# Two-block transformer step on one core: second output projection rescheduled, first gate/up pair by plain products

## The reference

```python
mixed = jnp.concatenate([rms_norm_2(attn, attn_out_norm[l]),
                         rms_norm_2(sgu, sgu_out_norm[l])], axis=-1)
y = mixed @ w_out[l]                       # 1024 x 1024 by 1024 x 1024
x = x + rms_norm_2(y, post_mix_norm[l])
h = rms_norm_2(x, pre_ffn_norm[l])
f = (jax.nn.silu(h @ w_gate[l]) * (h @ w_up[l])) @ w_down[l]   # D_FF = 2816
x = x + rms_norm_2(f, post_ffn_norm[l])
```

## Time and profile before

| | us |
|---|---|
| median of 3 runs (lowest to highest) | 2106.87 (2106.09 to 2108.21) |
| the profiled execution's own time | 2106.91 |
| its span, first to last instruction | 2105.1 |
| PE busy | 2011.8 (96% of the span) |
| DVE, POOL, ACT busy | 1333.3, 955.3, 844.4 |
| mean granted TensorE clock | 0.978 of full |

### The profile page before, as it was taken

How to read it: one execution, slowest core, us unless ns; L and a number is a source line. 1 busy time by engine, 2 the same in 40 slices (tenths; PEclk the granted TensorE clock), 3 DMA queues, 4 the chain that set the end, 5 groups by cost and what they waited for, 6 DMA issues and landing times.

```text
span 2105.1 us, 27422 instructions
## 1 busy us (share of the span) xinstructions
PE 2011.8 (96%) x10009; PEld 1667.0 (79%) x10009; DVE 1333.3 (63%) x1759; ACT 844.4 (40%) x1349; POOL 955.3 (45%) x566
## 2 busy tenths in 40 slices
PE   7999999999999999999998998876999999999997
PEld 6888888888887778888887798755888888878885
DVE  7887777665547554973512544797656565656977
ACT  5444444434420044650203765456333323324443
POOL 1344555323334397733541101776555555535552
PEclk8999999999999999999999999987999999999998
DMA  9223322111112152341112001022333233347344
GB/s 285 63 79 111 111 74 94 52 38 30 50 52 80 41 190 91 120 142 59 41 30 80 1 1 51 21 100 70 105 120 102 79 118 105 100 168 242 100 137 153
DMA packets 178924, 193.96 MB, mean 92 GB/s; under 512 B 9799, under 2 KB 122904, under 8 KB 178842
## 3 DMA queue, kind: packets, MB, share of 16 engines
q1 hardware_dynamic: 172420, 178.53, 26.8%
q10 hardware_dynamic: 6422, 14.37, 1.9%
HBM read 151.71 MB, written 41.16 MB: 92 GB/s over the span
## 4 chain that ended last, share of the span: by engine, by line
PE 78%; DVE 10%; ACT 5%; issue 4%; POOL 2%; DMA 1%; SPq 0%; DVEq 0%; ACTq 0%; POOLq 0%
PE psum L1491 7%; PE psum L1493 6%; PE psum L1492 6%; PE psum L960 6%; PE psum L962 6%; PE psum L961 6%; PE psum L1121 3%; PE psum L1402 3%; PE psum L1559 3%; PE psum L1561 3%; PE psum L1560 3%; PE psum L980 3%; PE psum L981 3%; PE psum L982 3%; PE psum L1391 2%
## 5 line engine op out<-in xcount | busy, mean ns | idle before, releaser
L756 POOL TENSOR_TENSOR w_hi<-w_raw,ones 128x1024 fp32r<-128x1024 f32 x60 | 149.2, 2487 | 481.5 <-PE psum L962 357.2
L960 PE MATMUL psum<-h_hi,w_hi 128*128 128x512 f32 x704 | 284.1, 404 | 0.0
L962 PE MATMUL psum<-h_hi,w_lo 128*128 128x512 f32 x704 | 274.8, 390 | 0.0
L961 PE MATMUL psum<-h_lo,w_hi 128*128 128x512 f32 x704 | 274.3, 390 | 0.0
L1591 ACT ACTIVATE arena<-psum 128x1024 f32<-128x1024 f32 (+7 forms) x135 | 100.8, 750 | 220.5 <-PE psum L962 135.3
L759 POOL TENSOR_TENSOR w_lo<-w_raw,w_hi 128x1024 fp32r<-128x1024 f32 x60 | 163.9, 2732 | 4.7
L961 PEld LDWEIGHTS psum<-h_lo,w_hi 128*128 128x128 f32 x704 | 132.4, 188 | 28.4 <-issue 2.6
L960 PEld LDWEIGHTS psum<-h_hi,w_hi 128*128 128x128 f32 x704 | 132.4, 188 | 28.4 <-issue 2.6
L962 PEld LDWEIGHTS psum<-h_hi,w_lo 128*128 128x128 f32 x704 | 132.1, 188 | 28.5
L1559 PE MATMUL psum<-w_hi,h_hi 128*128 128x512 f32 x308 | 121.5, 394 | 7.8 <-DVE h_lo L3032 5.1
L1560 PE MATMUL psum<-w_lo,h_hi 128*128 128x512 f32 x308 | 121.1, 393 | 0.0
(11 more groups left out here) (414 smaller groups left out, 5298.0 us busy)
## 6 DMA issues: line engine op xcount, KB each, us to landing
w_raw<-w_in SPq DMA_DIRECT2D x64, 512.0 KB, 3.9
act_op<-arena SPq DMA_DIRECT2D x77, 256.0 KB, 2.1
arena<-act_op SPq DMA_DIRECT2D x77, 256.0 KB, 2.7
w_raw<-w_gate SPq DMA_DIRECT2D x22, 512.0 KB, 4.0
w_raw<-w_up SPq DMA_DIRECT2D x22, 512.0 KB, 5.2
arena<-ada_w SPq DMA_DIRECT2D x16, 512.0 KB, 7.2
arena<-w_out SPq DMA_DIRECT2D x16, 512.0 KB, 5.6
out_T<-arena SPq DMA_DIRECT2D x16, 512.0 KB, 5.9
```

What stands on the lines that cost most here:

```text
L960: pe.matmul(o, wh, xh, start=(k == 0), stop=False)
L961: pe.matmul(o, wh, xl, start=False, stop=False)
L962: return pe.matmul(o, wl, xh, start=False, stop=(k == KT - 1))
```

## The change

It edits one stretch of the kernel, in six places.

1. **Attention scale.** The eight tiles are shared: DVE takes the even ones, ACT the odd ones. The root's table is loaded by ACT beforehand, and the first four B high parts go ahead of the wait for the attention output.
2. **B side eight places ahead.** `q_b2` has eight slots, ACT makes the B high part of step n+4 when it makes the A high part of step n. POOL's queue changes: T4 (four) and then S1 (four) both follow the low part of step 7, where S1 had been spread over steps 4 to 7 and T4 over 8 to 11; S4 moves from steps 18 to 21 to steps 22 to 25.
3. **A side order.** `Q_ORDER_A` makes the A parts of steps 26, 24, 27, 25 (operand A12, known early) between those of 16 and 20.
4. **Last two products tile by tile.** Steps 20 to 27 (P3 and P2) run per token tile: 12 matmuls of P3, then 12 of P2. Tile t then has C12 and C11 after 24 (t+1) matmuls.
5. **Norm of tokens.** New queues for ACT and DVE (`q_ms`, `q_rstd`, `q_xn`, `q_res`, `q_row`, `q_x`, `q_square`), with the norm row and the square of tiles 0 to 3 over all 1024 columns at once.
6. **First pair plainly.** The gate and up columns are multiplied without Strassen: 4 products g1, u1 (with B11, B21) and g2, u2 (with B12, B22), of 24 matmuls each, 96 in all where there were 84. The weights' sums S1 to S4 of the first pair go; those of the second pair are made by POOL. ACT rounds the first pair's weights. B12 gets a high and a low part of its own. T1 to T4 are made after that, and the second pair runs in the order `SECOND_PRODUCTS`.

The diff, cut to its core:

```diff
+SECOND_PRODUCTS = ["A11", "A12", "S4", "S2", "S1", "S3", "A22"]
-Q_POOL = {"T3": 0, "T2": QJ, "T1": 2 * QJ, "S3": 3 * QJ, "S1": 4 * QJ, "T4": 5 * QJ, "S4": 6 * QJ}
+Q_POOL = {"T3": 0, "T2": QJ, "T1": 2 * QJ, "S3": 3 * QJ, "T4": 4 * QJ, "S1": 5 * QJ, "S4": 6 * QJ}
+Q_ALL = QN - 2 * QJ
+Q_ORDER_A = list(range(17)) + [26, 17, 24, 18, 27, 19, 25, 20, 21, 22, 23]
         def q_b2(n):
-            return [h_lo[:, n % 4, e * HALF:(e + 1) * HALF] for e in range(2)]
+            return [h_lo[:, n % 8, e * HALF:(e + 1) * HALF] for e in range(2)]
# SP
-            raw_free(0)
+            sp.wait_ge(gp_done, NPR)
             load_pair(2, 0)
# POOL
-                if 4 <= n < 8:
-                    q_sum("S1", n - 4)
-                if 8 <= n < 12:
-                    q_sum("T4", n - 8)
-                if 18 <= n < 22:
-                    q_sum("S4", n - 18)
+                if n == 7:
+                    for i in range(QJ):
+                        q_sum("T4", i)
+                    for i in range(QJ):
+                        q_sum("S1", i)
+                if 22 <= n < 26:
+                    q_sum("S4", n - 22)
+            for a, name in enumerate(("A11", "A21", "A12", "A22")):
+                hi, lo = plain_w[name]
+                pool.wait_ge(gw_round, a + 1)
+                TT(lo, a_raw(name, 0), hi.bitcast(F32), ALU.subtract).then_inc(gw_ready, 4 if name == "A22" else 1)
...
+            for name in ("A11", "A12", "S4"):
+                second_lo(name)
+            t_lo(0, "T2", t2_raw)
+            t_lo(1, "T1", r11)
+            second_lo("S2")
+            second_lo("S1")
+            t_lo(2, "T3", r22)
+            second_lo("S3")
+            second_lo("A22")
+            t_lo(3, "T4", r21)
# PE
             for t in range(4):
-                for n in range(QN - O_TAIL, QN):
+                for n in range(Q_ALL, Q_ALL + QJ):
+                    if t == 0:
+                        q_operands(n)
+                    mm = q_out(n, n % QJ, t)
+                mm.then_inc(o_step, 1)
+                pe.wait_ge(o_sums, Q_C0 + O_C["C21"] + t + 1)
+                for n in range(Q_ALL + QJ, QN):
...
+            pe.wait_ge(gw_ready, 2)
             for k in range(4):
                 transpose_half(4, 1, [k + 4])
                 taken(T_BASE[4] + k + 1)
-                mm = gu_k("A11", k)
+                plain_k("g1", "A11", "B11", k, k == 0, False)
+                plain_k("u1", "A21", "B11", k, k == 0, False)
+            pe.wait_ge(gw_ready, NPR)
             for k in range(4):
                 taken(T_BASE[4] + 4 + k + 1)
+                mm = plain_k("g1", "A12", "B21", k, False, k == 3)
...
             b_transpose(0)
             b_transpose(1)
+            for k in range(4):
+                if k in (1, 2):
+                    b_transpose(k + 1)
+                pe.wait_ge(x_ready["B12"], k + 1)
+                pe.wait_ge(x_ready["B22"], k + 1)
+                plain_k("g2", "A11", "B12", k, k == 0, False)
...
# ACT
+            for t in range(1, NT, 2):
+                A(att_o[:, t, :], att_o[:, t, :], ACT.Identity, scale=rstd[:, t:t + 1]).then_inc(mixn_done, 1)
+            for n in Q_ORDER_A[4:]:
+                q_hi_a(n, O_PRODUCTS[n // QJ], n % QJ)
+                if n < 24:
+                    q_hi_b(n + 4, O_PRODUCTS[n // QJ + 1], n % QJ)
...
+            q_square(1)
+            q_square(2)
+            take_b11(mul, [0])
+            q_root(2)
+            take_b11(mul, [1])
+            q_square(3)
+            q_x(0)
+            q_x(1)
+            take_b11(mul, [2, 3])
+            q_root(3)
+            q_xn(3, 1, 3)
+            take_b11(mul, [4])
+            q_x(2)
+            plain_hi("A22")
+            take_b11(mul, [5])
+            q_root(4)
+            q_xn(4, 2, 2)
+            take_b11(mul, [6])
+            q_x(3)
+            take_b11(mul, [7])
+            q_root(5)
+            for name in ("A11", "A12", "S4"):
+                second_hi(name)
...
+                for e, (name, raw) in enumerate((("B12", r12), ("B22", r22))):
+                    A(x_hi[name][:, k, :], src, ACT.Identity, scale=mul(k + 4 * e)).then_inc(b22_taken, 1)
+                    A(raw[:, k, :], src, ACT.Identity, scale=mul(k + 4 * e)).then_inc(b22_taken, 1)
# DVE
+            for t in range(0, NT, 2):
                 TS(att_o[:, t, :], att_o[:, t, :], rstd[:, t:t + 1], None, ALU.mult).then_inc(mixn_done, 1)
...
+            for k in range(4):
+                dve.wait_ge(b22_taken, 4 * k + 4)
+                TT(r11[:, k, :], r12[:, k, :], r11[:, k, :], ALU.subtract).then_inc(t_sum, 1)
+                dve.wait_ge(t_sum, 2 * k + 1)
+                TT(t2_raw[:, k, :], r22[:, k, :], r11[:, k, :], ALU.subtract).then_inc(t_sum, 1)
```

More of the change, by code:

```diff
@@ L153, in q_hi @@
 def q_hi(n, of_b):
[L154 removed]
+    return Q_HI + Q_ROUNDED.index((n, of_b)) + 1
 def out_steps():
@@ L344, in q_a @@
         def q_a(n):
+            if n in (24, 25):
+                return [h_hi[:, 2 * n - 44 + e, HALF:] for e in range(2)]
             x = qa_ring[:, n % 4] if n < QN - 2 else qa_last[:, n - (QN - 2)]
@@ L2052, in _ @@
             act.dma_start(POST_ROW, ap["post_mix_norm_2"][0].partition_broadcast(P)).then_inc(row_in, 16)
-            q_hi_b(0, "P1", 0)
-            q_hi_b(1, "P1", 1)
+            A(lb_tmp, ones[:, 0:8], ACT.Sqrt)
+            for j in range(QJ):
+                q_hi_b(j, "P1", j)
+            act.wait_ge(ao_done, 2 * NT)
+            mix_square(att_o, 2 * NT - 1, NT - 1, NT - 1)
+            root(M_ATT)
             q_raw_copy(4)
@@ new lines, in _ @@
+            mul = lambda k: col("pre_ffn_norm_2", k)
+            for t in range(4):
+                out_square("C21", t, 4 + t, NT + 4 + t, 1)
+            q_root(0)
+            q_x(4)
+            q_x(5)
+            q_square(0)
+            for name in ("A11", "A21"):
+                plain_hi(name)
+            q_x(6)
+            q_x(7)
+            plain_hi("A12")
+            q_root(1)
+            q_xn(1, 4, 0)
+            q_xn(1, 5, 1)
+            q_square(1)
+            q_square(2)
@@ new lines, in _ @@
+            act.wait_ge(gp_done, 1)
+            A(silu_of[0], psum[:, P_BANK["g1"], :], ACT.Silu).then_inc(silu_a_done, 1)
+            for a, name, raw in ((2, "T2", t2_raw), (1, "T1", r11)):
+                for k in range(4):
+                    act.wait_ge(t_sum, 2 * k + a)
+                    copy(x_hi[name][:, k, :], raw[:, k, :]).then_inc(t_rounded, 1)
+            act.wait_ge(spilled[1], 16 * 2)
+            act.wait_ge(gp_done, 3)
+            A(u2_of[0], psum[:, P_BANK["g2"], :], ACT.Silu).then_inc(silu_b_done, 1)
@@ L2105, in _ @@
+            act.wait_ge(gp_done, NPR)
+            second_hi("S2")
+            second_hi("S1")
+            for k in range(4):
+                act.wait_ge(t_sum, 8 + k + 1)
+                copy(x_hi["T3"][:, k, :], r22[:, k, :]).then_inc(t_rounded, 1)
+            second_hi("S3")
+            second_hi("A22")
+            for k in range(4):
+                act.wait_ge(t_sum, 12 + k + 1)
+                copy(x_hi["T4"][:, k, :], r21[:, k, :]).then_inc(t_rounded, 1)
             act.dma_start(ROW_F, ap["post_ffn_norm_2"][0].partition_broadcast(P)).then_inc(row_in, 16)
@@ L2159, in _ @@
             each = [[name] for name in PRODUCTS]
-            gu_pair(0, 0, FIRST_PRODUCTS, [["A11"], [], ["S2"], ["S1"], ["S3"], ["A22", "A12"], ["S4"]], False)
-            gu_pair(1, 1, PRODUCTS, each, False)
+            gu_pair(1, 1, SECOND_PRODUCTS, [["A11"], [], [], ["S2"], ["S1"], ["S3"], ["A22", "A12", "S4"]], False)
             with act.Fori(1, FT // 2 - 1) as j:
```

427 lines of the change are left out of this document (241 added, 186 removed).

## The result

The changed kernel takes 2088.87 us (median of 4 runs, 2086.64 to 2091.67), beside 2107.32 us for the kernel before in 4 runs on the same chip: a ratio of 0.9914, 95% interval 0.9896 to 0.9931. In a second comparison it was 2087.47 us (5 runs) against 2105.94 us (9 runs): 0.9916, interval 0.9903 to 0.9930. The forecast was 2091.3 us, range 2083 to 2100. The profiled execution took 2087.27 us, span 2085.5.

The account below looks back on a forecast made before the run. The soft stretches ahead of PE's gapless run, with waits on DVE, POOL and ACT, were taken as the bound. Pair 2 moves from 1492.1 to 1476.5, 15.6 us: 2106.9 - 15.6 = 2091.3 us, range 2083 to 2100.

Parts of the forecast that it names:

- POOL's line of 21: POOL's 21 queued instructions ahead of the third gate/up pair, forecast at 34.0 us together, mean 1.62.
- a: Attention scale: four of eight tiles leave DVE, PE's 4.79 us wait goes, second transposes start at 1313.1 instead of 1318.13.
- b: Projection steps 3 to 20: S1 at 1325.0, step 8 at 1338.6, step 20 at 1374.0, 5.4 us gained.
- d: Projection end to first transposes of tokens 0 to 3: ACT and DVE need 25.2 us instead of 38.5, reaching 1421.9.
- c: Last two projection products: end at 1396.7 against 1402.6; PE's idle 6.46 us and half clock behind it go.
- e: B12 and B22 transposes, copies and low parts: 18.0 us, last B22 low part at 1439.9.
- f: From the last B22 low part to the third pair: POOL's queue sets 36.6 us, third pair at 1476.5.
- Rival 1: POOL less disturbed by DVE, 1.25 us for all 21 instructions ahead of the third pair: 2080 us; chance 0.13.
- rival 2: POOL and DVE exclude each other fully in projection steps and first pair: 4.3 us later, 2095.6 us; chance 0.12.
- rival 3: PE stays at half clock from the projection's end to the third pair: 2105 us; chance 0.05.
- rival 4: DVE-POOL port decides: POOL's 21 instructions at 2.28 us each ahead of the third pair, 2111 us; chance 0.05.
- rival 5: Early norm of tokens 4 to 7 is late, PE idles 6.5 us after the projection: 2098 us; chance 0.07.

Follow-up runs that it names:

- e_scale_dve: Changed kernel with the attention scaling undone, all eight tiles scaled by DVE again; 2093.48 us.
- the repeat: The changed kernel run again as it is, beside two further versions; 2087.47 us.
- e_lo_twice: Changed kernel with POOL making each of the four low parts of T2 twice; 2094.89 us.
- e_t2_early: Changed kernel with DVE's T1 and T2 sums moved into the loop of the B12 and B22 low parts, ACT and POOL following; 2081.51 us.
- e_lo_dve: Changed kernel with the eight low parts of T3 and T4 made by DVE instead of POOL; 2087.66 us.
- e_product_order: Changed kernel with the tile order undone: P3 finished for all four tiles, then P2 for all four; 2092.2 us.
- e_four_places: Changed kernel with B split four steps ahead again for steps 0 to 23, A in natural order, new order of POOL's sums kept; 2108.81 us.

## Why the prediction was right

The total was forecast 2.4 us too high against the median, 4.0 against the profiled execution. Of the latter 1.9 are the down projection, 2.1 lie ahead of pair 2. The mechanism held where the forecast stood on it: the waits went that were to go, and POOL's line of 21 set pair 2. In a, b and d the time came out for reasons that were in part wrong.

**a.** The wait went, as forecast. The transposes came at 1316.07 and not 1313.1: step 0 followed a wait of 3.30 us (2.25 before) and its 12 matmuls took 0.43 each, which is 12 x 0.2 = 2.4 us. The term of 24 x 0.227 = 5.4 us "as before" was 8.1. DVE's four tiles took 5.78 us (1.45 each, not 1.17) and ended at 1315.1. At full clock PE would have waited for them, so the late transposes had two causes, one under the other.

**b.** Step 8 within 0.3 us, by luck in the mechanism: "S1 is there at 1325.0. From it DVE alternates" should have read that DVE gets to S2 at 1325.06 from its own copies out of the transposes. The 3.40 us a step behind that is as forecast. The wrong chain is why I gave the scaling 0 to 2 us in `e_scale_dve` and it was worth 6.7. The waits at steps 20 and 23 were 0.61 and 1.68, in sum 2.3 for 3.6; the upper bound of 4.4 for the first should have been 15.0 - 10.9 = 4.1.

**c, d.** The marks are right: end 0.2 us early, transposes at once, then 24.8 us for 25.2. Inside d sizes cancelled: ACT had seven squares (7.6 us) where five (6.2) were counted, its three stops were 2.0 us and not the estimated 5.0, and from the last root to the transposes it took 2.7 us for 1.2. The wait for the A22 weights was listed as 0.93 us, 2.60 in the repeat, and pair 2 is the same within 0.1: it costs nothing, as said.

**e.** 16.9 us for 18.0; half clock for nine matmuls only, and the transposes ahead of them at full clock. Before, this part took 18.8 us by its marks (1441.12 to 1459.93), not 18.3.

**f.** The term on which the forecast stood: 36.3 us for 36.6, 21 instructions in 34.2 us for 34.0. `e_lo_twice`, `e_t2_early` and `e_lo_dve` each moved pair 2 as POOL's line says. One slip is in the sum: 1.70 - 1.25 is 0.45 us a subtraction and not 0.43, which makes the line 34.4 us.

Rival 1 (POOL undisturbed), whose 2080 us also lay outside the range that was to take in most of it, falls with 1.63 us a mean instruction, rival 2 (full exclusion) with periods of 1.70, rival 3 with a clock of 0.86, rival 4 with the same 1.63, rival 5 with the transposes at 1396.49; `e_product_order` shows what it would have cost, 3.6 us for the 6.5 I had put.

What each part is worth, undone alone: scaling 6.7 us, eight places (with POOL's order and that of A) 9.2 to 10.4, tile order 3.6, A order about 1.4. They overlap, since each was undone in the presence of the others, and their sum is no share-out of 17.7. The new order of the norms and the plain multiplication of the first pair were not undone. So the 13.7 us between the projection's end and tokens 0 to 3, the largest part of the gain, are read from the timelines, and how they divide among these two and the tile order is not shown.

## What to carry to other kernels

When a line of low parts on one engine ends last, look at where the line begins, before its instructions: here a sum made one loop earlier filled the idle time ahead of it and gave 7.7 us, while a shorter wait and a warmer PE added to it gave 0.2. A ring's depth and the order in which an in-order engine serves it are one design: the new order with the old depth gave the whole gain back (pair 2 at 1492.72). And judge an edit by the distance between two marks around it as well as by the total, since a wait far away from it moved the total by up to 4 us. Then look at the clock between the marks too: 1.6 us of clock hid what the order of the A parts costs.

## What the runs showed of the hardware

DVE's scaling of a 128x512 tile loses about 1 us beside POOL, nearly as much as a subtraction between two SBUF tiles does. These are its four instructions, grouped (duration in ns, least, median and greatest), in `e_four_places`, where POOL worked until 1311.9 and then stood idle:

```profile
L3028 DVE TENSOR_SCALAR arena<-arena,st x4: 474/476/1494, 1310.7 to 1312.9; 128x512 f32<-128x512 f32 x4
```

One began beside POOL and took 1.49 us, the three others 0.47 to 0.48, less than the 0.68 of a subtraction of the same size. In the changed kernel the four take 5.78 us, 1.45 each, and POOL never stops there. A subtraction between two SBUF tiles goes from 0.60 us from start to start (`e_four_places`, 1313.27, POOL idle) to 1.70 (changed kernel, 1326.75 to 1328.45). The Trainium skill, page "SBUF — State Buffer", section "Who interferes with whom", says that `tensor_scalar`, which this scaling is, can run in a mode that uses two ports and then contends with GpSimd; both durations agree with that. I had taken the 1.17 of the kernel before, a mixture of the two. DVE's subtractions with one input in PSUM kept their 0.68 us beside POOL.

The length of a wait alone does not tell which clock PE has behind it. In the down projection all kernels have the same code and PE waits once for POOL. The 40 us behind the wait hold 178 matmuls after 2.42 us, 177 after 2.67, 170 after 2.69, 169 after 3.09 and 163 after 3.20. That looks like a rule, but two other kernels break it: after 3.18 us (`e_t2_early`) and 2.73 us (`e_scale_dve`) the clock was 1.00 throughout, after 2.71 us (`e_lo_twice`) it was 0.96. The same holds ahead of g2, where one wait of 2.60 us left PE at half clock in seven kernels and at full clock in three. From the end of the wait in the down projection to the end of the span it took 210.5 us in the changed kernel, 212.4 in the kernel before and 213.9 in `e_lo_dve`. What decides it these runs do not show.
